# Experts' block of a streaming encoder step: order of the weight loads, the zero stores and the last tail stores on the SP queue

## The reference, cut to what matters

```
def hier_moe(h, lp):
    ...
    lg = (t @ lp["w_router_group"] + lp["b_router_group"]).astype(jnp.float32)
    pg = jax.nn.softmax(lg, axis=-1)
    gi = jnp.argmax(lg, axis=-1)
    ...
    top_v, top_i = lax.top_k(jax.nn.softmax(le, axis=-1), TOP_K)
    wts = pg_top * top_v / jnp.sum(top_v, axis=-1, keepdims=True)
    ...
    for e in range(N_EXPERTS):
        hid = jax.nn.silu(t @ lp["w_expert_gate"][e]) * (t @ lp["w_expert_up"][e])
        out = out + comb[:, e:e + 1] * (hid @ lp["w_expert_down"][e])
```

## Time and profile before

| what | value |
|---|---|
| median of 3 runs | 1783.12 us |
| the three runs | 1774.79, 1783.71, 1783.12 us |
| profiled execution, its own time | 1775.52 us |
| its span in the trace | 1773.8 us |
| mean granted TensorE clock | 0.917 |
| PE busy | 1503.5 us (85%) |
| experts' block in the trace | 1086.47 to about 1656.9 us |
| combine block in the trace | 1656.95 us to the end |
| weight loads of experts | 20 of 2048 KB for each of gate, up, down |

### The profile page before, as it was taken

The page is one execution under the profiler, slowest core; times in us unless marked ns, Lnnn a source line. Parts: engine busy times, 40 slices in busy tenths (PEclk is TensorE's granted clock), DMA queues, the critical chain, the costliest instruction groups (busy, mean ns, idle before and its releaser), DMA issues. The chain is left out here.

```text
span 1773.8 us, 29923 instructions
## 1 busy us (share of the span) xinstructions
PE 1503.5 (85%) x12585; PEld 1096.1 (62%) x12585; DVE 547.6 (31%) x1006; ACT 384.8 (22%) x774; POOL 184.4 (10%) x281
## 2 busy tenths in 40 slices
PE   5899999999939999999999984699999999995100
PEld 3566665666628778776877652678878788683000
DVE  4254464302115545454545324110000000000066
ACT  5332223112113323332332220011111111100022
POOL 0011111100022001110111000100000000000031
PEclk9899999999969999999999966699999999997655
DMA  7345654422163321332132005997777877948563
GB/s 297 112 142 192 224 210 162 150 74 74 50 216 115 96 62 38 96 97 61 38 96 67 1 30 201 398 342 260 284 287 257 309 262 261 321 160 299 83 203 128
DMA packets 184095, 299.54 MB, mean 169 GB/s; under 512 B 22519, under 2 KB 94491, under 8 KB 183965
## 3 DMA queue, kind: packets, MB, share of 16 engines
q1 hardware_dynamic: 166860, 240.96, 39.7%
q0 software_dynamic: 12928, 42.79, 6.9%
q10 hardware_dynamic: 4176, 13.90, 2.0%
HBM read 241.96 MB, written 55.64 MB: 168 GB/s over the span
## 5 line engine op out<-in xcount | busy, mean ns | idle before, releaser
L2048 PE MATMUL banks<-moe_xT,moe_wg 128*128 128x160 f32 x1024 | 146.0, 301 | 0.8 <-ACT moe_xT L2168 0.8
L2048 PEld LDWEIGHTS banks<-moe_xT,moe_wg 128*128 128x128 f32 x1024 | 140.3, 190 | 7.6 <-issue 6.6
L2048 PE MATMUL banks<-moe_xT,moe_wu 128*128 128x160 f32 x1024 | 144.3, 299 | 0.0
L2048 PEld LDWEIGHTS banks<-moe_xT,moe_wu 128*128 128x128 f32 x1024 | 140.8, 190 | 0.0
L1215 PE MATMUL banks<-mixer_w_out,mixer_yT 128*128 128x512 f32 (+1 forms) x288 | 127.5, 601 | 4.5 <-DVE mixer_yT L1661 3.7
L598 PE MATMUL banks<-xT,w_v 128*128 128x352 f32 (+1 forms) x384 | 118.7, 469 | 0.0
L598 PE MATMUL banks<-xT,w_r 128*128 128x352 f32 (+1 forms) x384 | 118.6, 469 | 0.0
L598 PE MATMUL banks<-xT,w_k 128*128 128x352 f32 (+1 forms) x384 | 118.3, 468 | 0.0
L1471 POOL TENSOR_TENSOR mixer_LTm<-mixer_LT,level 128x256 f32<-128x256 f32 (+1 forms) x90 | 72.1, 825 | 407.3 <-ACT mixer_LTo L1527 282.3
L2089 PE MATMUL banks<-moe_wd,moe_hid 128*128 128x512 f32 x256 | 112.5, 592 | 0.0
L598 PEld LDWEIGHTS banks<-xT,w_v 128*128 128x128 f32 x384 | 72.6, 190 | 45.2 <-issue 2.2
(11 more groups left out here) (431 smaller groups left out, 2042.5 us busy)
## 6 DMA issues: line engine op xcount, KB each, us to landing
moe_wg<-w_expert_gate SPq DMA_DIRECT2D x20, 2048.0 KB, 9.2
moe_wu<-w_expert_up SPq DMA_DIRECT2D x20, 2048.0 KB, 11.8
moe_wd<-w_expert_down SPq DMA_DIRECT2D x20, 2048.0 KB, 10.0
w_mod<-w_ada SPq DMA_DIRECT2D x8, 2048.0 KB
mixer_feats<-feature_major SPq DMA_DIRECT2D x16, 768.0 KB, 8.4
wada<-w_ada SPq DMA_DIRECT2D x4, 2048.0 KB, 19.9
w_mod<-w_ada_final SPq DMA_DIRECT2D x4, 2048.0 KB
mixer_feats<-feature_major SPq DMA_DIRECT2D x8, 1024.0 KB, 5.8
```

What stands on the lines that cost most here:

```text
L2048: mm = pe.matmul(bank[:, i * S_STATIC:(i + 1) * S_STATIC], wt[:, u, q, (t0 + i) * P:(t0 + i + 1) * P], xT[:, e % 2, q, :], start=q == 0, s ...
```

## The change

On SP the 22 DMAs of zeros and final rows move from ahead of load 2 to ahead of load 5. After load 17 the loop of overflow passes, with its weight loads, comes before the last two `tail_out`. On POOL the wait for `rows_made` and the first overflow gather move from gather 4 to gather number 12 (`main_tile(9)`). On DVE the product of the final rows moves from behind expert 1 to behind expert 6. No work is added or removed, and PE's and ACT's instructions stay as they are.

```
@@ -1926,7 +1926,7 @@
                 load(None, bass.ds(e, 1), u, before)
 
             for s in range(NE + 2):
-                if s == 2:
+                if s == 5:
                     sp.wait_ge(sg("zero_made"), 1)
                     for i in range(NPASS):
                         sp.dma_start(d["y"][(T_OVER + i) * P:(T_OVER + i + 1) * P, :], xTo[:, :, :].rearrange("p k n -> p (k n)")).then_inc(sg("y_zeroed"), 16)
@@ -1947,9 +1947,9 @@
                 for u in range(2):
                     load_over(2 * k + u, u, sp.to_reg(2 * k + NE + u - 1))
 
+            passes(sp, step)
             tail_out(O_SET)
             tail_out(O_SET + 1)
-            passes(sp, step)
             for u in range(2):
                 sp.wait_ge(sg(f"ytail{u}_stored"), 4 * 16 * NE // 2)
             sp.sem_inc(sg("tails_out"), 1)
@@ -1989,7 +1989,7 @@
                 if kind == "main":
                     tail(e - 1)
                 take(i)
-                if i == main_tile(3):
+                if i == main_tile(9):
                     pool.wait_ge(sg("rows_made"), 2)
                     take_over(T_OVER)
             tail(NE - 1)
@@ -2405,7 +2405,7 @@
             place_main(0)
             for e in range(NE):
                 expert(e)
-                if e == 1:
+                if e == 6:
                     dve.wait_ge(sg("rows_loaded"), 112)
                     for r in range(2):
                         V.scalar_tensor_tensor(final_rows[:, r, 1, :], final_rows[:, r, 1, :], 1.0, xgo[:, :], ALU.add, ALU.mult).then_inc(sg("rows_made"), 1)
```

## The result

The changed kernel took 1750.09 us in the median of 4 runs (1748.34 to 1754.09), against 1783.1 us before (1774.79 to 1783.71). The ratio is 0.9833, with a 95% interval of 0.9802 to 0.9865. The forecast was 1751 us in a range of 1741 to 1763.

A forecast was written before the change was run, and what follows sets the result against it. PE bounds the middle of the experts' block, so transfers cost time only at its two ends: 22.5 + 5.4 = 27.9 us. Off the profiled execution 1747.6, off the median 1755.2; forecast between them, 1751 us, range 1741 to 1763.

The forecast's parts named there:

- The end: Second overflow pass, weights issued ahead of the tail stores: takes the first pass's 25.1 us, 22.5 us gone (20.3 to 23).
- The start: First gather before expert 0, zeros no longer ahead of it: lands after 4.4 us, not 9.8; 5.4 us gone (0 to 5.6).
- The tail stores: Block's end on SP: eight stores behind the loop, ACT waits for them with at least 10 us in hand; cost 0.
- The 22 transfers: Zeros and rows ahead of load 5: 34.2 us of transfers, load 5's margins 6.6, 5.9 and 14 us; cost 0.
- Rivals 2 and 5: At load 5: backlog over 40 us, 1757 to 1760, chance 0.08; backlog below half rate, slower than before, chance 0.01.
- POOL and DVE: Overflow gather and final rows' product moved later: gather wanted only five experts after its issue, cost 0.
- Rival 1: Block's start: the first gather's 9.8 us is its own cost there, start term about 0, time 1756; chance 0.12.
- Rivals 3 and 4: Block's end: its tail moves to SP, 1758, chance 0.04; loop's weights still issued after expert 15, 1770 or 1778, chance 0.03.

The follow-up runs named there:

- the repeat: The changed kernel, unaltered, run once more on the same chip as its two halves: 1753.23 us in the median of 4 runs, ratio to before 0.9871.

## Why the prediction was right

**The end, 22.5 us.** Measured 22.4. Reading the first overflow pass as what the second would be was exact to 0.1 us, as the two issue the same instructions and in both the weights are now there in time. The loss was more than the named waits, and the clock's part of it came back too. (The term's low end of 20.3 doesn't follow from its conditions: 22.5 less 2 is 20.5, and 18.5 of waits less 2 is 16.5. It was a guess.) The half with only this edit has the same 25.2 us pass.

**The start, 5.4 us.** The mechanism held: the landing went from 9.8 to 4.8 us (4.4 was predicted), since nothing stood behind load 1, and with the zeros back in their place PE's wait was 10.3 us again, with the landing at 9.6. The size was off by the clock. I took it that expert 0 starts 4.96 us after the first turn and runs as before. In five executions of the table the product ran cold, and 1.5 to 2.4 us were lost in it; four of them began it as early as I said or nearly. The term is 5.6 us where expert 0 is warm as in before (the repeat, and the loop that ends early), and 2.6 to 3.6 where it isn't; it is 3.3 in the profiled execution after. The prediction used the clock for the end of the block and left it out at the start, although the row was there: the earlier trace rows has a granted clock of 0.64 from 1100 to 1150 us.

**The tail stores, 0.** Right, with 20.5 us in hand instead of the 10 that I called the least.

**The 22 transfers, 0.** Right, and the times came out near: the transfers took 33.9 us where 34.2 was predicted; gate of load 5 predicted in at 1267.3 and measured 1267.3, up 1272.5 against 1274.0, down 1277.7 against 1280.3. The first agreement is in part luck, as this execution's block began 2.8 us later and PE was 3.3 us earlier in it. The margin of the up was 3.9 us, not 5.9. Rivals 2 and 5 fell with the 33.9 us, far under the 40 that they needed; with the zeros doubled the transfers still ran near 400 GB/s. The limit of about 358 GB/s in the Trainium skill, "DMA: Bandwidth & Descriptors", section "Bandwidth", is by its own words the share of a core when both cores of a pair stream. One core runs here, so the 401 GB/s of the earlier trace rows didn't contradict the page, and the page was no argument against the change.

**POOL and DVE, 0.** No wait for the overflow gather or the final rows appeared in after.

**Rival 1** (a gather that is slow by itself) fell with the landing of 4.8 us. **Rivals 3 and 4** fell with SP's rows above.

**The median.** The forecast put 1751 between the sum off the profiled execution and the sum off the median. The measured medians are 1750.09 and 1753.23. That the first lies within 1 us of the forecast is in part luck: the medians differ by 33.0 us in the first set of runs, where the sum was 27.9 and the block in the trace gives 25.7, and by 26.2 in the second, where the block gives 28.0. Only single executions were traced, so where the rest of the medians' difference lies isn't shown. The stretches that the change doesn't touch can hold it: the experts' block began anywhere between 1086.5 and 1098.7 us in ten profiled executions, with the same code ahead of it. The latest of these, the run with only the loop moved, took 1766.85 us, 12 us above its own median, with a block as short as expected. What makes that spread stays open.

## What to carry to other kernels

On a queue that issues in order, a small store that waits for the last result holds back every large load behind it: put the loads whose buffers are free first, if nothing reads the store soon. A block of transfers without a due time goes where PE has a lead of weights, and its room there is the landing time against the time PE wants the next load. In the one run that went beyond it, the excess was paid about one for one, and PE's clock added its part. Where a loop has an undisturbed turn and a disturbed one, the undisturbed one is a good price for the repair: 25.1 us was read there, and 25.2 measured. And a stage that begins with stores of single elements is worth a look: moving two of them gave more than the start term of this change.

## What the runs showed of the hardware that was not expected

The clock's rise doesn't follow PE's work by a fixed time. In before the first product was warm 4.96 us after PE's first turn; in after it was still at 0.63 on average 4 to 10 us behind its first turn; and one and the same kernel showed both. The Trainium skill, "TensorE: Matmul & The Clock Gate", section "Part 1: The HAM clock gate (the "warmup" mystery)", says that the number of cold matmuls varies from run to run; the spans of 4.6 and 6.3 us for the same 32 matmuls agree.

Two stores of 6.5 KB, made of single elements of 4 bytes, held up the gathers behind them: in the window of 1634 to 1640 us of after the transfers are busy 0.41 of the time and move 2 GB/s, and the first gather of the combine block lands 24.0 us after its issue. With these stores elsewhere it lands after 6.0 us, and ACT's wait for it is 19 us shorter.

```profile
1634.00:1640.00 6.00, 0.00 (x0) 0.00 (x0) 0.00 (x0) 1.28 (x1) 3.73 (x7) 0.50 0.41 2
1640.00:1646.00 6.00, 0.00 (x0) 0.00 (x0) 0.00 (x0) 0.00 (x0) 0.49 (x1) 0.50 1.24 23
```
